# Scattering the gates of 256 tokens instead of 128 into the gate matrix by indirect DMAs in a one-core decoder block

## The reference

```python
q = (xt @ wq).reshape(t, PEER_HEADS, 2, PEER_HALF_DIM)
sc = jnp.einsum('thpc,hpnc->thpn', q, sub_keys)
top_v, top_i = lax.top_k(sc, PEER_TOPK)
...
best_v, best_pos = lax.top_k(cand_v, PEER_TOPK)
expert = jnp.take_along_axis(cand_id, best_pos, axis=-1)
gate = jax.nn.softmax(best_v, axis=-1)
...
hc = jnp.einsum('cd,chkd->chk', xc, u[ec])
ac = gc * jax.nn.gelu(hc)
out = jnp.einsum('chk,chkd->cd', ac, v[ec])
```

## Time and profile before

| what | value |
|---|---|
| median of three runs | 3308.53 us (3305.33 to 6432.45) |
| profiled execution, its own time | 3301.1 us |
| its span, first to last instruction | 3299.3 us |
| TensorE matmul busy | 3180.3 us, 96% |
| VectorE busy | 2431.3 us, 74% |
| ScalarE busy | 1078.1 us, 33% |
| GpSimd busy | 659.4 us, 20% |
| mean granted TensorE clock | 0.988 |

### The profile page before, as it was taken

The page is one execution under the profiler, slowest core; times in us unless marked ns, Lnnn a source line. Parts: engine busy times, 40 slices in busy tenths (PEclk is TensorE's granted clock), DMA queues, the critical chain, the costliest instruction groups (busy, mean ns, idle before and its releaser), DMA issues.

```text
span 3299.3 us, 46895 instructions
## 1 busy us (share of the span) xinstructions
PE 3180.3 (96%) x17074; PEld 2965.8 (90%) x17074; DVE 2431.3 (74%) x3461; ACT 1078.1 (33%) x1379; POOL 659.4 (20%) x464
## 2 busy tenths in 40 slices
PE   7999999999997879999999999999999999999997
PEld 5777778899997779999999999999999999999785
DVE  6544443599977968888887888888888888885644
ACT  4224422222233533333333333333332333333422
POOL 3120000066673111112111121111212111110200
PEclk9999999999998999999999999999999999999998
DMA  4243122344566668888788887888878788863322
GB/s 147 81 153 111 67 84 94 105 112 112 114 187 216 232 238 286 291 285 302 266 291 287 279 306 265 293 282 279 302 270 297 277 286 291 283 238 117 102 90 100
DMA packets 249394, 694.46 MB, mean 210 GB/s; under 512 B 35824, under 2 KB 93680, under 8 KB 213360
## 3 DMA queue, kind: packets, MB, share of 16 engines
q1 hardware_dynamic: 189424, 418.77, 37.0%
q0 software_dynamic: 55296, 268.53, 24.0%
q10 hardware_dynamic: 4608, 6.29, 0.5%
HBM read 657.79 MB, written 35.72 MB: 210 GB/s over the span
## 4 chain that ended last, share of the span: by engine, by line
PE 73%; DVE 16%; DMA 4%; issue 4%; ACT 2%; POOL 1%; DVEq 0%; SPq 0%; ACTq 0%
PE bank L486 23%; PE bank L488 23%; PE bank L487 23%; DVE w_lo L1203 4%; DMA raw<-in_u_t 3%; DVE one_ij L1548 2%; DMA raw<-in_v 1%; ACT w_hi L875 1%; DVE row L1526 1%; PE bank L578 1%; PE bank L601 1%; PE bank L579 1%; POOL gate_matrix L1790 1%; DVE x_lo L1659 1%; DVE x_lo L1220 1%
## 5 line engine op out<-in xcount | busy, mean ns | idle before, releaser
L486 PE MATMUL bank<-x_hi,w_hi 128*128 128x384 f32 (+1 forms) x3024 | 1079.8, 357 | 35.8 <-DVE x_lo L1220 16.7
L488 PE MATMUL bank<-x_hi,w_lo 128*128 128x384 f32 (+1 forms) x3024 | 1069.9, 354 | 0.0
L487 PE MATMUL bank<-x_lo,w_hi 128*128 128x384 f32 (+1 forms) x3024 | 1069.8, 354 | 0.0
L875 ACT ACTIVATE w_hi<-raw 128x1024 fp32r<-128x1024 f32 (+1 forms) x668 | 688.3, 1049 | 887.7 <-DMA raw<-in_v 336.7
L1203 DVE TENSOR_TENSOR w_lo<-raw,w_hi 128x1024 fp32r<-128x1024 f32 (+1 forms) x668 | 802.9, 1219 | 210.0 <-ACT w_hi L875 200.3
L486 PE MATMUL bank<-a_hi,w_hi 128*128 128x384 f32 x2048 | 687.6, 336 | 14.3 <-DVE w_lo L1203 11.1
L487 PE MATMUL bank<-a_lo,w_hi 128*128 128x384 f32 x2048 | 685.8, 335 | 0.0
L488 PE MATMUL bank<-a_hi,w_lo 128*128 128x384 f32 x2048 | 685.8, 335 | 0.0
L486 PEld LDWEIGHTS bank<-x_hi,w_hi 128*128 128x128 f32 x3024 | 571.4, 189 | 85.4 <-DVE w_lo L1203 16.8
L487 PEld LDWEIGHTS bank<-x_lo,w_hi 128*128 128x128 f32 x3024 | 571.9, 189 | 38.8 <-issue 1.2
L488 PEld LDWEIGHTS bank<-x_hi,w_lo 128*128 128x128 f32 x3024 | 571.0, 189 | 38.9
(11 more groups left out here) (198 smaller groups left out, 2049.5 us busy)
## 6 DMA issues: line engine op xcount, KB each, us to landing
raw<-in_u_t SPq DMA_DIRECT2D x256, 512.0 KB
raw<-in_v SPq DMA_DIRECT2D x256, 512.0 KB
g_tile<-gate_matrix SPq DMA_DIRECT2D x32, 768.0 KB
raw<-in_w_o SPq DMA_DIRECT2D x32, 512.0 KB
raw<-in_w_q SPq DMA_DIRECT2D x32, 512.0 KB
gate_matrix<-g_blk SPq DMA_DIRECT2D x8, 2048.0 KB, 7.4
raw<-in_w_gate SPq DMA_DIRECT2D x32, 512.0 KB
raw<-in_w_in SPq DMA_DIRECT2D x26, 512.0 KB
```

The costliest lines, as they stand in the source:

```text
L486: pe.matmul(out, w_hi[slot][:, blk, :], m_hi, start=first, stop=False)
L487: pe.matmul(out, w_hi[slot][:, blk, :], m_lo, start=False, stop=False)
L488: return pe.matmul(out, w_lo[slot][:, blk, :], m_hi, start=False, stop=last)
L875: act.activation(w_hi[slot][:, 8 * s:8 * s + n, :], raw[s][:, 0:n, :], ACT.Copy)\
```

## The change

The gates of the first 256 tokens (`PUT_T = 2` tiles of 128) are put by indirect DMAs, 32 per query head instead of 16, 256 in all. The one-hots make only those of the third tile: `ONE_TB` goes from 8 to 4 blocks. The number of plain spilled units, `ALONE`, goes from 11 to 15, so that all 32 spilled units are still computed. 16 zero stores of 1 MB are made instead of 8. `cell` and `put_gate` hold two tiles and lie at other addresses. GpSimd's order becomes: the puts of heads 0 to 4 (160), rows 0 and 1, then for rows 2 to 11 four puts and a row, for rows 12 to 15 eight puts and a row, and then the last 24 puts. The loops over blocks, now short, are written out. ScalarE no longer waits for `gates_put` ahead of the blocks.

```diff
-ALONE = 11
+ALONE = 15
...
-PUT_TB = P // TB
+PUT_T = 2
+PUT_TB = PUT_T * P // TB
...
-                if n - 2 < 2 * PUT_TB:
-                    b, half = divmod(n - 2, 2)
-                    sp.dma_start(g_dram[b, :, 64 * half:64 * half + 64, :],
-                                 zeros[:, :].rearrange("p (i t) -> p i t", t=TB)).then_inc(zeros_stored, 16)
+                if n - 2 < PUT_TB:
+                    for half in range(2):
+                        sp.dma_start(g_dram[n - 2, :, 64 * half:64 * half + 64, :],
+                                     zeros[:, :].rearrange("p (i t) -> p i t", t=TB)).then_inc(zeros_stored, 16)
...
-            sp.wait_ge(gates_put, 16 * TOPK * PH)
+            sp.wait_ge(gates_put, 16 * PUT_T * TOPK * PH)
...
-            act.wait_ge(gates_put, 16 * TOPK * PH)
             for s in range(2):
                 g_block(s, s)
-            with act.Fori(1, ONE_TB // 2 - 1) as b2:
-                for s in range(2):
-                    act.wait_ge(g_stored[s], 16 * b2)
-                    g_block(2 * b2 + s, s)
...
-                dve.tensor_tensor(of_head(put_gate), b_exp[:, 0, :], b_inv[:, 0:1].to_broadcast([P, TOPK]), ALU.mult)
+                for t in range(PUT_T):
+                    dve.tensor_tensor(of_head(put_gate[:, t]), b_exp[:, t, :], b_inv[:, t:t + 1].to_broadcast([P, TOPK]),
+                                      ALU.mult)
...
-                step(dve.tensor_tensor(of_head(cell), pair_e[:, 0, :], pair_e[:, 1, :], ALU.add))
+                for t in range(PUT_T):
+                    ins = dve.tensor_tensor(of_head(cell[:, t]), pair_e[:, 0, t, :], pair_e[:, 1, t, :], ALU.add)
+                step(ins)
...
+            def put_gate_of(n):
+
+                hd, t, k = n // (PUT_T * TOPK), n // TOPK % PUT_T, n % TOPK
+                if n % (PUT_T * TOPK) == 0:
+                    pool.wait_ge(topk_step, PER_TOPK * (hd + 1))
+                    if hd:
+                        pool.wait_ge(gates_put, 16 * n)
+                pool.indirect_dma_start(g_dram.rearrange("b j i t -> (b j i t)").unsqueeze(1),
+                                        bass.IndirectOffsetOnAxis(ap=cell[:, t, hd, k:k + 1], axis=0),
+                                        put_gate[:, t, hd, k:k + 1], None, compute_op=ALU.add)\
+                    .then_inc(gates_put, 16)
...
             pool.wait_ge(zeros_stored, 16 * 2 * PUT_TB)
-            for hd in range(PH - 1):
-                put_gates(hd)
+            for n in range(5 * PUT_T * TOPK):
+                put_gate_of(n)
             pool.wait_ge(topk_step, PER_TOPK * PH)
             pool.wait_ge(rows_out, 4)
             for k in range(2):
                 load_row(k)
-            put_gates(PH - 1, rows=2)
-            for k in range(5, EARLY - ONE_TB + 1):
+            n = 5 * PUT_T * TOPK
+            for k in range(2, EARLY):
+                for m in range(4 if k < EARLY - ONE_TB else 8):
+                    put_gate_of(n + m)
+                n += 4 if k < EARLY - ONE_TB else 8
                 load_row(k)
-            for b in range(ONE_TB):
-                if b and b + EARLY - ONE_TB < EARLY:
-                    load_row(b + EARLY - ONE_TB)
+            for m in range(n, PH * PUT_T * TOPK):
+                put_gate_of(m)
```

More of the change, by code:

```diff
@@ L111, in build_block @@
         gain = at("gain", rest + 2 * K, [P, N_GAIN])
-        rope_c = at("rope_c", rest + 2 * K + 320, [P, 3])
+        rope_c = at("rope_c", rest + 2 * K + 320, [P, 2 + PUT_T])
         p_inv = at("p_inv", rest + 2 * K + 352, [P, 4, 16])
@@ L163, in build_block @@
         sel = [at(f"sel{i}", one + (42 + 2 * i) * K, [P, TC, PH, TOPK]) for i in range(3)]
-        pair_e = at("pair_e", one + 59 * K, [P, 2, TOPK])
-        cell = at("cell", one + 59 * K + 512, [P, PH, TOPK], U32)
-        put_gate = at("put_gate", one + 60 * K, [P, PH, TOPK])
+        pair_e = at("pair_e", one + 59 * K, [P, 2, PUT_T, TOPK])
+        cell = at("cell", rest + 17 * K + 576, [P, PUT_T, PH, TOPK], U32)
+        put_gate = at("put_gate", rest + 18 * K + 576, [P, PUT_T, PH, TOPK])
         t_v = [at(f"t_v{i}", one + 48 * K + 256 * i, [P, TC, TOPK]) for i in range(2)]
@@ L426, in store_block @@
                 sp.dma_start(g_dram[b + PUT_TB], g_blk[s][:, :, :]).then_inc(g_stored[s], 16)
-            with sp.Fori(0, ONE_TB // 2 - 2) as b2:
-                for s in range(2):
[L430 to L436, removed]
+            for b in range(ONE_TB):
+                if b + ALONE + 2 < U_PEER - U_ALONE:
+                    load_unit(U_BLOCK + b + 2, packed(u_t, spilled(2 * (PH - 1) + ALONE + b + 2)))
+                else:
+                    load_unit(U_BLOCK + b + 2, packed(u_t, U_BLOCK + b + 2 - U_PEER))
+                store_block(b, b % 2)
             for s in range(2):
                 sp.wait_ge(g_stored[s], 16 * (ONE_TB // 2))
-            sp.wait_ge(gates_put, 16 * TOPK * PH)
+            sp.wait_ge(gates_put, 16 * PUT_T * TOPK * PH)
             sp.wait_ge(spill_stored, 16 * N_GROUPS)
@@ L749, in _ @@
             for i in range(3):
-                for t in range(1, TCD):
+                for t in range(PUT_T, TCD):
                     mm = pe.transpose(bank[i][:, t * P:(t + 1) * P],
@@ L788, in _ @@
             g_block(1, 1)
-            with pe.Fori(1, ONE_TB // 2 - 1) as b2:
-                for k in range(2):
-                    g_block(2 * b2 + k, k)
             g_block(ONE_TB - 2, 0)
@@ L1068, in _ @@
                         act.wait_ge(hk_turned, i + 1)
-                        act.activation(hk_t[:, i, P:TD], bank[i][:, P:TD], ACT.Copy).then_inc(hk_ready, 1)
+                        act.activation(hk_t[:, i, PUT_T * P:TD], bank[i][:, PUT_T * P:TD], ACT.Copy).then_inc(hk_ready, 1)
             def g_evict(b, s, q):
@@ L1481, in keys_and_gates @@
                 dve.scalar_tensor_tensor(of_head(expert), i_of[:, TCD, :], float(NK), j_of[:, TCD, :], ALU.mult, ALU.add)
-                dve.scalar_tensor_tensor(pair_e[:, 0, :], j_of[:, 0, :], float(NK * TB),
-                                         rope_c[:, 2:3].to_broadcast([P, TOPK]), ALU.mult, ALU.add)
-                step(dve.tensor_scalar(pair_e[:, 1, :], i_of[:, 0, :], float(TB), None, ALU.mult))
-                step(dve.tensor_tensor(of_head(cell), pair_e[:, 0, :], pair_e[:, 1, :], ALU.add))
+                dve.scalar_tensor_tensor(pair_e[:, 0, :, :], j_of[:, 0:PUT_T, :], float(NK * TB),
+                                         rope_c[:, 2:2 + PUT_T].unsqueeze(2).to_broadcast([P, PUT_T, TOPK]),
+                                         ALU.mult, ALU.add)
+                step(dve.tensor_scalar(pair_e[:, 1, :, :], i_of[:, 0:PUT_T, :], float(TB), None, ALU.mult))
+                for t in range(PUT_T):
+                    ins = dve.tensor_tensor(of_head(cell[:, t]), pair_e[:, 0, t, :], pair_e[:, 1, t, :], ALU.add)
+                step(ins)
             lo(U_WQ + 1, (U_WQ + 1) % 2)
@@ L1548, in one_hots @@
                 dve.tensor_tensor(one_ij[s][:, :, :, :], iota[:, None, None, :].to_broadcast(o),
-                                  hk_t[:, 0:2, bass.ds(OH * q + P, OH)].unsqueeze(3).to_broadcast(o), ALU.is_equal)\
+                                  hk_t[:, 0:2, bass.ds(OH * q + PUT_T * P, OH)].unsqueeze(3).to_broadcast(o), ALU.is_equal)\
                    .then_inc(oh_ij, 1)
@@ L1552, in one_hots @@
                 dve.tensor_tensor(one_g[s][:, :, :], one_ij[s][:, 0, :, :],
-                                  hk_t[:, 2, bass.ds(OH * q + P, OH)].unsqueeze(2).to_broadcast([P, OH, NK]), ALU.mult)\
+                                  hk_t[:, 2, bass.ds(OH * q + PUT_T * P, OH)].unsqueeze(2).to_broadcast([P, OH, NK]), ALU.mult)\
                    .then_inc(oh_g, 1)
@@ L1858, in _rope_columns @@
     phase = np.repeat(np.array([np.pi / 2, np.pi / 2, np.pi, 0.0]), 32)
-    return np.stack([np.tile(freq, 4), phase, np.arange(P) // TB * float(P * NK * TB) + np.arange(P) % TB], 1).astype(np.float32)
+    return np.stack([np.tile(freq, 4), phase, np.arange(P) // TB * float(P * NK * TB) + np.arange(P) % TB,
+                     (np.arange(P) // TB + P // TB) * float(P * NK * TB) + np.arange(P) % TB], 1).astype(np.float32)
 def _pool_inverse():
```

## The result

The changed kernel takes 3414.6 us at the median against 3306.9 us of the kernel before (its median with a fourth run): ratio 1.033, 95% interval 1.0314 to 1.0345. (One run of each, of 7032.02 and 6432.45 us, was disturbed and is left out of the ratio.) It is slower. Its profiled execution has a span of 3411.1 us, 111.8 more than before.

A forecast was written before the change was run, and what follows sets the result against it. GpSimd's 256 puts were taken to become the bound from the second head on, releasing SyncE at 1302 instead of 1188.9: 113 - 3 + 1 + 1 = +112 us on 3301.1, plus 4 for the median, 3416 us; range 3365 to 3455.

The forecast's parts named there:

- What is removed: Block stretch: four of eight blocks replaced by four plain units, at most 45 us saved, 1.4% of the time.
- Heads 0 to 3: Query heads, VectorE busy: 128 puts at 2.28 us plus three landing waits of 2 us, 298 us, to 969.
- Head 4: After VectorE's heads, VectorE standing in row_dot(0): 32 puts at 2.1 us plus 2, 69 us, to 1038.
- Eight puts and a row beside one-hots: Rows 12 to 15 on GpSimd: four times eight puts at 2.6 us and a row, 97 us, to 1249.
- the port rule of the prediction: One-hot stage: some VectorE instructions lock the shared SBUF port, delaying GpSimd's DMA descriptors; without dearer puts 87, not 97 us.
- The last 24 puts: End of GpSimd's puts, VectorE done: 24 at 2.1 us plus 2, 52 us; SyncE passes at about 1302.
- some 3 us sooner: -3 us: Start of the product stage: earlier unit loads long done, so the raw load after g_tile goes 3 us sooner.
- The +1 for the slow clock: Start of the product stage: TensorE comes out of a long stop at a lower clock, +1 us allowed.
- The zero stores: Head stage: eight added 1 MB stores behind the weight loads, +1 us; without cover up to 6.3 us each.
- Fast puts once VectorE stands still: Rival: from 969 us on every put takes 1.85 us, +51 us, 3355 us in all; chance 0.09.
- The puts keep up: Rival: all 256 puts at 1.85 us, SyncE released at 1187, 3302 us in all; chance 0.03.
- Dearer meeting: Rival: puts at 3.65 us through the one-hots (+34), landing waits of 4.4 us (+17), 3467 us; chance 0.08.

The follow-up runs named there:

- e6_half_wide: The changed kernel with the second tile's puts only 64 partitions wide (gates of tokens 192 to 255 left out), still 256 puts: 3378.9 us, ratio 1.0222.
- e7_hold_rows: The changed kernel with GpSimd holding the gathers of rows 16 and on until the first g_tile has landed: 3405.7 us, ratio 1.0292.
- e2_extra_puts: The kernel before with each put made a second time into a scratch tensor, in the change's GpSimd order: 3431.2 us, ratio 1.038.
- e3_rows_first: The changed kernel with rows 0 and 1 after 128 puts, three or six puts ahead of later rows, more puts at the end: 3414.5 us, ratio 1.0332.

## Why the prediction was right

The forecast of 3416 us stands against 3414.6, and the direction and the mechanism are as argued. That it is so close is luck: SyncE was released 7 us early and the rest took 7 us more than laid out, and within the release the first heads were 9 us long and later steps short.

- **What is removed: right.** 45 us forecast; the run with 128 puts has 51 us at SyncE's release. Its 1.5% is well clear of no change (0.9834 to 0.9868), so the prediction's 2% as the least that can be told was too coarse.
- **Heads 0 to 3: 9 us too short.** GpSimd was through with them at 978.7, not 969. The three waits between heads took 10.2 us (3.27, 2.20 and 4.71) where 6 had been laid out, and a put 2.33 us where the earlier trace rows gave 2.28. That pace was measured where GpSimd had pauses between heads. Without them the gaps before a put were longer: twelve, of 1.8 to 4.9 us, 38.9 us in 128 puts, where the kernel before has ten, 26.2 us in 112.
- **Head 4: right.** After a landing wait of 2.27 us its 32 puts took 64.2 us (980.66 to 1044.81), 2.00 each; together 66, where 69 had been laid out with 2.1 a put and 2 us of wait. VectorE stood in `row_dot(0)` for 84.6 us, 75 forecast.
- **Four puts and a row: right.** 109.3 us from 1047.40 to 1156.66, 110 forecast.
- **Eight puts and a row beside one-hots: right in kind, 8 us long.** 89.2 us instead of 97. Less the four row loads (7.8 us and 1.2 of gaps), a put took 2.51 us, 2.6 had been taken, and 2.00 was measured where VectorE stood still. This is the difference that the port rule of the prediction asked for, and the ends of the long puts (see e6_half_wide) show it put by put. The rows themselves met a one-hot only half of the time (2.52, 1.36, 2.53, 1.36 us).
- **The last 24 puts: 49 us, 52 forecast.** SyncE passed at 1294.95 instead of 1302, 7 us early.
- **Behind it: the term that was mis-sized.** The step "some 3 us sooner: -3 us" came out as +3.3 us (38.5 against 35.2). It looked at when SyncE could issue the load, and took the row gathers to start "behind the last put as they did behind the last block"; but they start 1.3 us ahead of `g_tile`, not 0.7 behind it. ScalarE began the unit's second half 19.4 us behind `g_tile`, where it was 16.2, and e7_hold_rows shows that the gathers do it. The +1 for the slow clock was not needed on this chain: from VectorE's end of U_PEER+3 to the scaling of its product passed 11.0 us in both kernels. The other 2.5 us lie in the product stage and are no more than executions differ.
- **The zero stores: free.** A head took 16.5 us, with the DMA share at 0.45, and the first put started no later (670.82, before 671.07); +1 us had been allowed.
- **The rivals.** "Fast puts once VectorE stands still" was half true, 2.00 in the stop itself, but it needed 1.85 everywhere. "The puts keep up" fell by the pace and by e2_extra_puts. "Dearer meeting" fell at 2.51 against its 3.65: a put that begins with such an instruction does take 3.2 us, but 13 of 32 met none and others caught only its tail.

## What to carry to other kernels

An engine at 20% busy may have no room where the work is to go: lay the new instructions on its own clock from the moment their inputs exist to the moment their results are needed, at the pace of whole groups of them (2.33 us here beside a busy VectorE, where the median instruction is 1.55). Here some 176 puts would have fitted, by estimate, and 256 were asked for, and each one too many cost 2 us, whether TensorE's idle time lay before the blocks or behind them. Where many small indirect DMAs go out back to back, count instructions, not bytes, and look for a gap that comes after a fixed number of them.

## What the runs showed of the hardware

- The descriptor space of GpSimd's DMAs sets a wait where puts follow one another: with 4096 bytes a partition after every 15th put of 128 descriptors, with 2048 after every 7th, 1.9 to 2.1 us each while the rest is idle, up to 4.9 us in the changed kernel beside unit loads and a busy VectorE.
- A put that begins while VectorE runs an instruction with two inputs in SBUF ends 1.41 to 1.44 us behind that instruction's end (19 of 19 long puts beside the one-hots), so it takes up to 3.3 us instead of 1.55. A `tensor_reduce` beside it left it at 1.55 us.
- A put of 64 descriptors takes 1.42 us and one of 128 takes 1.55 us, while a gather of 128 rows of 8 KB takes 0.94 us to issue. What makes the put dearer than the gather, its accumulation or its scattering direction, wasn't tried.
- Four 1 MB gathers issued around SyncE's `g_tile` kept a 1 MB load back by 10 us. In that trace the issue of two SyncE transfers took 8.1 us instead of 1.6, but in e3_rows_first it took 3.2 and the load was as late.
